# Projections that start before the norm is known: x times the norm's weights goes in, 1/rms scales what comes out

## What is computed

```python
def rms_norm(x, w):
    y = x * rsqrt(mean(x * x, axis=-1) + NORM_EPS)
    return y * w

# a hybrid layer (first block, twice)
z = rms_norm(x, norm_mix_w) @ w_in + b_in
ya = dilated attention of rope(z[q]), rope(z[k]), z[v]
yb = sigmoid(z[mo]) * normed(mlstm(silu(conv(z[mq, mk])), z[mv], z[mi], z[mf]))
x = x + (sigmoid(z[ga]) * (ya @ w_proj_att) + sigmoid(z[gb]) * (yb @ w_proj_mlstm)) @ w_out
x = x + square(relu(rms_norm(x, norm_mlp_w) @ w_ff1)) @ w_ff2

# the layer of the second block, on x = rms_norm(x, final_norm_w)
p = rms_norm(x, norm1_w) @ w_in            # z, xbc, dt, q, k, v, qi, ki, wi, u, gates
y_ssd = rms_norm(ssd(silu(conv(p[xbc])), softplus(p[dt])) * silu(p[z]), ssd_norm_w)
y_att = attention over the top 128 keys that qi, ki, wi choose
y_pool = windowed means of p[u], mixed
x = x + (sum of sigmoid(gates) * (y @ w_up)) @ w_out
hn = rms_norm(x, norm2_w);  a, b = split(hn @ w_ffn_in)
out = rms_norm(x + (silu(a) * b) @ w_ffn_out, final_norm_w)
```

## Time and profile before

| | |
|---|---|
| median of the runs | 2765.41 us (2763.36 to 2765.75, 3 runs) |
| the profiled execution | 2763.08 us, span 2761.3 us |
| mean granted clock of PE | 0.963 |
| busy: PE, DVE, ACT, POOL | 2640.0, 1102.0, 873.8, 955.9 us |
| HBM read and written | 213.81 and 2.10 MB, 78 GB/s |

### The profile page before, as it was taken

One profiled execution on the slowest core, in us unless ns is written; L12 is line 12 of the kernel. 1 busy time (PEld: TensorE's weight loads), 2 busy tenths in 40 slices (PEclk: granted clock), 3 DMA queues, 4 the chain that ended last, 5 costly groups with the idle time before them and its releaser, 6 DMA issues. The chain is left out here.

```text
span 2761.3 us, 30509 instructions
## 1 busy us (share of the span) xinstructions
PE 2640.0 (96%) x12181; PEld 2105.6 (76%) x12181; DVE 1102.0 (40%) x1490; ACT 873.8 (32%) x1087; POOL 955.9 (35%) x207
## 2 busy tenths in 40 slices
PE   7999999999998999899999998989899999999998
PEld 6757688788886857688788887778776588788887
DVE  3345543440513245544440422166666524322202
ACT  4245233321322245333331322352323423322212
POOL 2313234344442312334244443352232144344441
PEclk7999999999998999999999998999899999999999
DMA  3212122223322211122223322221111122223221
GB/s 130 77 31 75 59 81 92 76 91 100 99 91 70 92 31 62 61 77 92 76 91 97 101 91 77 77 77 54 52 61 61 50 92 92 77 92 105 91 98 54
DMA packets 176245, 217.90 MB, mean 79 GB/s; under 512 B 7564, under 2 KB 156996, under 8 KB 176132
## 3 DMA queue, kind: packets, MB, share of 16 engines
q1 hardware_dynamic: 175364, 215.66, 24.3%
q10 hardware_dynamic: 768, 0.66, 0.1%
HBM read 213.81 MB, written 2.10 MB: 78 GB/s over the span
## 5 line engine op out<-in xcount | busy, mean ns | idle before, releaser
L262 POOL TENSOR_TENSOR w_lo<-w_raw,w_hi 128x2048 fp32r<-128x2048 f32 x203 | 955.7, 4708 | 1765.7 <-ACT w_hi L253 1765.7
L253 ACT ACTIVATE w_hi<-w_raw 128x2048 fp32r<-128x2048 f32 x203 | 387.9, 1911 | 644.4 <-PE ps L1543 341.4
L292 PE MATMUL ps<-h_hi,w_hi 128*128 128x512 f32 x960 | 373.5, 389 | 0.0
L293 PE MATMUL ps<-h_lo,w_hi 128*128 128x512 f32 x960 | 373.5, 389 | 0.0
L294 PE MATMUL ps<-h_hi,w_lo 128*128 128x512 f32 x960 | 373.5, 389 | 0.0
L628 PE MATMUL ps<-h_hi,w_hi 128*128 128x512 f32 (+2 forms) x760 | 329.2, 433 | 1.3 <-issue 1.3
L628 PE MATMUL ps<-h_hi,w_lo 128*128 128x512 f32 (+2 forms) x760 | 302.9, 399 | 0.0
L628 PE MATMUL ps<-h_lo,w_hi 128*128 128x512 f32 (+2 forms) x760 | 302.2, 398 | 0.0
L292 PEld LDWEIGHTS ps<-h_hi,w_hi 128*128 128x128 f32 x960 | 180.2, 188 | 37.6
L294 PEld LDWEIGHTS ps<-h_hi,w_lo 128*128 128x128 f32 x960 | 180.2, 188 | 37.4
L293 PEld LDWEIGHTS ps<-h_lo,w_hi 128*128 128x128 f32 x960 | 180.2, 188 | 37.3
(11 more groups left out here) (404 smaller groups left out, 4134.4 us busy)
## 6 DMA issues: line engine op xcount, KB each, us to landing
w_raw<-in_w_in SPq DMA_DIRECT2D x74, 1024.0 KB, 5.2
w_raw<-in_w_ff SPq DMA_DIRECT2D x64, 1024.0 KB, 5.2
w_raw<-in_w_ffn_in SPq DMA_DIRECT2D x22, 1024.0 KB, 5.1
w_raw<-in_w_out SPq DMA_DIRECT2D x12, 1024.0 KB, 5.0
w_raw<-in_w_ffn_out SPq DMA_DIRECT2D x11, 1024.0 KB, 4.8
w_raw<-in_w_proj_att SPq DMA_DIRECT2D x4, 1024.0 KB, 5.2
w_raw<-in_w_proj_mlstm SPq DMA_DIRECT2D x4, 1024.0 KB, 5.0
w_raw<-in_w_up_ssd SPq DMA_DIRECT2D x4, 1024.0 KB, 5.1
```

Of the source, the lines that this page charges most:

```text
L253: act.activation(k.whi[:, slot * SLOT:(slot + 1) * SLOT], k.wraw[:, slot * SLOT:(slot + 1) * SLOT], ACT.Copy).then_inc(k.hi_done, 1)
L262: pool.tensor_tensor(k.wlo[:, a:a + SLOT], k.wraw[:, a:a + SLOT], k.whi[:, a:a + SLOT], ALU.subtract).then_inc(k.split, 1)
L292: pe.matmul(out, k.whi[:, w], xh(i), start=i == 0, stop=False)
L293: pe.matmul(out, k.whi[:, w], xl(i), start=False, stop=False)
```

## The change

Ten things, of which the first four are the core.

1. `Hand` takes the place of `Stats` and `Norm`. When a tile of x is final, ACT writes h_hi = x * w straight from it (L363) and its square (L373), and DVE writes h_lo = x * w - h_hi (L367). 1/rms is no part of h.
2. The squares of the eight tiles are added up on DVE (L381), through a PSUM bank. Four matmuls sum the one tile that is left, and one spreads 1/rms. Both are issued inside the side work that follows (`hooks`), not ahead of it. The spread result is kept as `rstd`, in the layout of tokens along columns, and as `rtok`, with tokens on partitions.
3. The lead unit is `fm_lead` (L316): 32 matmuls that need only h_hi, then the 16 with h_lo.
4. Evictions multiply by `rstd` or `rtok` on DVE. Where there is a bias or a tanh, it is a second instruction on ACT (`post`), which waits for DVE's. An MLP's `Up` takes relu times rstd out of PSUM on DVE and squares on ACT. `Glu` scales both halves on DVE and does silu on ACT in place.
5. `TwoNorms` does the two norms between the blocks at once: h_hi is x times the product of both weights, and the second mean square is a weighted sum of the same squares. `FirstNorm` scales x itself by the first norm, eight instructions on DVE ahead of the second block's conv.
6. `LastNorm` multiplies x by w as its tiles come; 1/rms goes on with the copies of the turned result.
7. `Project` is gone. q, k, v and the second block's conv inputs are side jobs like the others.
8. The loop, the clearing of semaphores and the barrier are gone: both layers are written out, and semaphores count on.
9. Setup: parameters are loaded and turned first; the four loads of x are issued by ACT. The bias of v is added to the attention's result, and the token biases are loaded from ACT's queue.
10. The ones of `mv` are written only where they are needed.

The number of units stays 203, and the budgets of the side work stay as they are. The core of the diff:

```diff
-class Stats(Stage):
-    def sum(self, pe, t):
-        pe.wait_ge(self.sem("squared"), t + 1)
-        for i in range(TT):
-            mm = pe.matmul(k.ps[:, self.bank, i:i + 1], self.slot(t)[:, i * P:(i + 1) * P], k.ones(P, 1), ...)
-class Norm(Stage):
...
+class Hand(Stage):
+    def hi(self, act, t):
+        act.wait_ge(*self.tile(t))
+        act.activation(self.k.hh(t), self.x(t), ACT.Copy, scale=self.w(t)).then_inc(self.sem("hi"), 1)
+    def lo(self, dve, t):
+        dve.wait_ge(*self.at("hi", t + 1))
+        dve.scalar_tensor_tensor(self.k.hl(t), self.x(t), self.w(t), self.k.hh(t), ALU.mult, ALU.subtract)\
+           .then_inc(self.sem("lo"), 1)
+    def add(self, dve, n):
+        t, ps = self.order[n], self.k.ps[:, self.ACC, :]
+        dve.wait_ge(*self.at("squared", max(t, self.seed) + 1))
...
+        out = self.acc if n == KD - 2 else ps
+        dve.tensor_tensor(out, ps, self.sq[t], ALU.add).then_inc(self.sem("added"), 1)
+    def sums(self, pe):
+        pe.wait_ge(*self.at("added", KD - 1))
+        for i in range(TT):
+            mm = pe.matmul(k.ps[:, self.SUMS, i:i + 1], self.acc[:, i * P:(i + 1) * P], k.ones(P, 1), ...)
...
+def fm_lead(k, pe, u, kt, cols, hand, outs, done):
+    for i in range(kt):
+        pe.wait_ge(*hand.at("hi", i + 1))
+        for c, out in enumerate(outs):
+            pe.matmul(out, k.whi[:, w], k.hh(i), start=i == 0, stop=False, skip_group_check=True)
+            pe.matmul(out, k.wlo[:, w], k.hh(i), start=False, stop=False, skip_group_check=True)
+    for c, out in enumerate(outs):
+        for i in range(kt):
+            if c == 0:
+                pe.wait_ge(*hand.at("lo", i + 1))
+            mm = pe.matmul(out, k.whi[:, w], k.hl(i), ...)
...
     def emit_out(self, who, eng, upto):
...
+                if job.post:
+                    eng.wait_ge(*self.read(job))
+                    job.post(eng).then_inc(self.sem("post"), 1)
...
     def conv_in(t):
-        return Job("act", lambda act, bank: act.activation(
-            cv[:, a:a + T], k.ps[:, bank, :], ACT.Identity, bias=k.col(B1 + 12 + t)), c=t % UT)
+        return biased(cv[:, a:a + T], t, B1 + 12 + t)
+    def scaled(dst, c, post=None):
+        return Job("dve", lambda dve, bank: dve.tensor_tensor(dst, k.ps[:, bank, :], rstd, ALU.mult), c=c % UT,
+                   post=post)
+    def biased(dst, c, bcol):
+        return scaled(dst, c, lambda act: act.activation(dst, dst, ACT.Identity, bias=k.col(c0 + bcol)))
...
     # Up, on ACT and on DVE
-            act.activation(r, k.ps[:, 2 * j:2 * j + 2, :].rearrange("p a b -> p (a b)"), ACT.Relu)\
-            dve.tensor_tensor(f, r, r, ALU.mult).then_inc(self.sem("f"), 1)
+            dve.scalar_tensor_tensor(r.rearrange("p (a b) -> p a b", b=T), k.ps[:, 2 * j:2 * j + 2, :], 0.0, rstd,
+                                     ALU.max, ALU.mult).then_inc(self.sem("r"), 1)
+            act.activation(f, r, ACT.Square).then_inc(self.sem("f"), 1)
...
+class FirstNorm(Stage):
+        for t in range(KD):
+            dve.scalar_tensor_tensor(h.x(t), h.x(t), h.w1(t), self.k.ps[:, h.FIRST, :], ALU.mult, ALU.mult)\
...
-            with nc.Fori(0, DEPTH) as l:
-                emit(k, first_layer(k, l, A))
+        x, angles = first_steps(k, A, table, st)
+        for l in range(DEPTH):
+            x = first_layer(k, l, A, st, x, angles)
+        second_layer(k, A, out, st, x)
+        emit(k, st)
```

More of the change, by code:

```diff
@@ L356, in act @@
     def act(self, act):
         k = self.k
[L358 to L362, removed]
+        if self.ahead is not None:
             hi_unit(k, act, self.ahead, 0)
-        act.wait_ge(self.sem("summed"), KD)
-        act.activation(k.root[:, 0:TT], k.ps[:, self.bank, 0:TT], ACT.Sqrt, bias=k.eps[:, 0:1],
+        act.activation(k.eps[:, 4:5], k.eps[:, 0:1], ACT.Sqrt)
+        act.wait_ge(*self.at("sums", 1))
@@ L366, in act @@
+        act.activation(k.root[:, 0:TT], k.ps[:, self.SUMS, 0:TT], ACT.Sqrt, bias=k.eps[:, 0:1],
                        scale=1.0 / D).then_inc(self.sem("root"), 1)
[L367 to L379 removed]
+        act.wait_ge(*self.at("recip", 1))
@@ L546, in unit @@
     def unit(self, src, kt, cols, xh, xl, jobs):
         u = units(self.k, 1)
+        lead = not self.units
         self.units.append((u, src, cols))
@@ L550, in unit @@
             job.n, job.u, job.kt, job.cols, job.xh, job.xl = len(self.jobs), u, kt, cols, xh, xl
-            job.last = job is jobs[-1]
+            job.last, job.lead = job is jobs[-1], lead
+            if job.n < 4:
+                job.need = [*job.need, self.before.tile(job.n)]
             if not job.last:
@@ L1230, in up @@
                 t = j * (w // P) + c
-                waits = [self.read(self.gates[t])] + (list(free) if t == 0 else [])
+                waits = [self.posted(self.gates[t])] + (list(free) if t == 0 else [])
                 if add:
@@ L1586, in dve @@
             if c < KD - 1:
[L1587 removed]
+                dve.wait_ge(*self.at("tile", c + 1))
             else:
@@ L2655, in second_layer @@
     dt_rows = k.at("s_dt_rows", o_scr + T, T)
-    dt_at = plain(DT2, SH, [Job("act", lambda act, bank: act.activation(
-        dt_rows[0:SH, :], k.ps[0:SH, bank, :], ACT.Copy), c=0, rows=SH)])
+    for j in range(6):
+        xbc_at = plain(XBC2 + j * UC, UC, [copy(xbc3[:, t, CONV - 1:], t % UT) for t in (2 * j, 2 * j + 1)])
+    side.hooks = {side.jobs[2].end: [hand.sums], side.jobs[3].end: [hand.spread]}
+    dt_at = plain(DT2, SH, [Job("dve", lambda dve, bank: scaled(dve, dt_rows[0:SH, :], bank, slice(0, SH)),
+                                c=0, rows=SH)])
     for j in range(4):
```

1537 lines of the change are left out of this document (821 added, 716 removed).

## The result

The changed kernel takes 2689.8 us (median of 4 runs, 2685.0 to 2691.7), the one before 2764.4 beside it: ratio 0.973, 95% interval 0.971 to 0.974. That is 75 us less where 89 were forecast; 2689.8 lies inside the range, 15 us above the forecast. The profiled execution took 2689.5 us with a span of 2687.7, so 73.6 us less than the span before.

The account below looks back on a forecast made before the run. PE was taken as the bound, its own sums and half clock at norms outweighing waits; 113 us gained at the norms less 24 lost in the middle gave 89, so 2675 us, eight times in ten 2645 to 2712.

Parts of the forecast that it names:

- Three norms before an MLP: Norms in both first layers and once in the second block: few sums left on PE, 39 us gained in all.
- End of layer 0: Norm after the first layer: 24.2 us of cost falls to 1.9 us of sums and spread, 22.3 us gained.
- Between the blocks: Two successive norms costing 40.4 us: 3.8 of sums and spreads and 1.8 of PE's wait stay, 34.8 us gained.
- Start: Kernel's beginning: lead unit ends at 45 instead of 53.2, 6.3 us gained, bounds 0 to 15.
- End: After the last product: turning back the result needs only x times w and begins at once, 11 us gained.
- lead units that don't run ahead: Rival: slots come free late, so five norms each wait 4.5 us for POOL's w_lo; 22 less gain, 2696 us, chance 0.08.
- evictions that POOL slows: Rival: about 120 moved evictions each cost 0.90 us more on DVE, kernel slower at 2782 us, chance 0.04.
- Rope: Two evictions on DVE ahead of the rotation PE waits for: 1.4 us lost per layer.
- The rest of the layers: Per layer, three output-gate evictions between conv taps lose 2.1 us, and some eight mLSTM gate evictions about 3.2.
- SSD: Four evictions in the tail of this second-block stage, on a wait of 4.5 us: 2.8 us lost.
- Attention and pooling: Second block's attention and pooling stretch: evictions moved to DVE would lose only 1 us.
- DVE's chains become the second bound: Rival: longer PE waits in rope, gates, mLSTM and conv, some followed by half clock; loss 50, 2700 us, chance 0.22.

## Why the prediction was right, and where it was off

- **PE's work and clock around the norms bound the kernel: right.** The waits as a whole didn't fall, and the gain is PE's busy time, 77.5 us. That the second half of a norm is dear through sums and the lower clock was shown by putting the sums back: 50 us.
- **Three norms before an MLP**, 39: measured 13.4, 13.4 and 11.8. The lo parts met POOL more often than foretold, once in each of the three norms and not once in all, but behind 32 products without h_lo that cost little: all six waits for h_lo come to 1.9 us.
- **End of layer 0**, 22.3: measured 22.3. The clock of 1.00 came as foretold.
- **Between the blocks**, 34.8: measured 35.1, with a wait of 1.50 where 1.8 was taken.
- **Start**, 6.3: measured 4.2. The second unit does start at 45.14 as foretold (53.17 - 45.14 = 8.0, less 1.9 for sums and spread), but PE then waits 1.90 us once more, for DVE's qk at 59.94. That the start came out as said is in part luck: the angles met both w_lo, a case that I had priced at no gain, and their operations were cheaper than my 0.7 us, most of them 0.43. Where rope begins, 2.8 us are left of it.
- **End**, 11: measured 12.0. Together the norms gave 112, with 113 forecast. The rivals on this side, lead units that don't run ahead and evictions that POOL slows, were wrong: the 56 gate evictions took 685 and 687 ns on average, by the groups below, and of all evictions with 1/rms the 26 that ran beside a w_lo took 671 to 693 ns, the 97 others 669 to 694.
- **Rope**, 1.4 per layer: measured 1.25. **The rest of the layers**, 5.3 each: measured 3.7 and 1.8. The eight evictions of the mLSTM cost nothing; its stretch is even 2.4 us shorter in both layers. What was lost came from elsewhere. From the forget gates to the softplus 2.9 us went in each layer: ACT's second pass over the output gates now waits for DVE, so its w_hi is late and PE waits for POOL's w_lo. And the attention took 3.1 and 1.3 us more. In the first layer that is the clock behind the longer wait of rope, 3.4 us for 2.2; the same place, after and before:

```profile
138.00:144.00 6.00, 6.00 (x15) 3.35 (x15) 2.19 (x8) 1.53 (x6) 0.00 (x0) 0.67 0.00 0
```

```profile
135.00:141.00 6.00, 6.00 (x22) 3.29 (x23) 2.30 (x11) 2.39 (x7) 0.00 (x0) 1.00 0.10 5
```

  The second layer's 1.3 are within the 2.8 us that came and went there without an edit.
- **Second conv**, 3.9: measured 0.8, since the scalings lay beside other work.
- **SSD**, 2.8: mis-sized, measured 6.2. The evictions were 2, and three, not four, stood in the tail; 4.2 was the collision of DVE's scaling with a w_lo that ACT's free time had moved there.
- **Gates in the rounds of top-k**, 3: measured 2.9.
- **"Attention and pooling, 1"**: this is the step that failed, with 23.3 us. I had counted how long the evictions take. But an eviction on DVE also waits for its products, and behind it, in order, stood the pooling that PE waits for; so late, it also met two w_lo with PE out of other work. Two experiments that take this meeting away give back 21 us each.

The groups of moved evictions, of the kernel after (busy, mean ns of one):

```profile
L1330 DVE TENSOR_TENSOR gate<-ps,rstd 128x512 f32<-128x512 f32 x32 | 21.9, 685 | 56.2 <-PE ps L706 56.2
L1330 DVE TENSOR_TENSOR s_gate<-ps,cos 128x512 f32<-128x512 f32 x24 | 16.5, 687 | 67.1 <-PE ps L706 65.6 <-issue 1.5
```

The losses come to 2.5 + 5.5 + 0.8 + 6.2 + 2.9 + 23.3 = 41.2, and putting the evictions back gives 40.6, an agreement that is part chance, since the stages differ. 112 - 41 = 71 stands against the measured 73.6 of the spans; some 3 us I can't place. The rival "DVE's chains become the second bound" came as near as my forecast, with a loss of 50 and 2700 us, 10 from the measured time where mine was 15 off. But it named rope, gates, mLSTM and conv, and these took 9 us of the loss.

## What to carry to other kernels

When an eviction moves to another engine, its 0.7 us is the smaller price: ask which products it waits for, and what stands behind it on that engine that the bound engine is waiting for. Here three such evictions, 2.1 us by their length, cost 22 us. Put evictions of side work behind the main chain's group, not ahead of it. And look for small matmuls on the bound engine first, since here they cost their own time and the clock of what followed.

## What the runs showed of the hardware

- The granted clock fell from 1.00 to 0.50 while PE did nothing but one-column fp32 matmuls, with no idle time in the rows; it was 1.00 again after 512-column products had followed. The prediction named two waits ahead of the low clock of the earlier trace rows; that such sums bring it down without a wait was not in it.
- Beside a w_lo on POOL, DVE operations on SBUF alone took 4.6 to 4.9 us instead of 0.43 and 0.69, also one with a single tile as input (L1907); one on 128x16 numbers (L2292, below) took 4.40 instead of 0.17. Evictions, with an operand in PSUM, took 0.69 there as elsewhere. The Trainium skill (SBUF — State Buffer, SBUF: two separate sides) names two kinds of VectorE operation, one with two SBUF inputs and one in a 2-port mode, that share a pair of ports with GpSimd, so that the later one is blocked until the first has finished. I had used only the first half of it. L1908 and L2292 have two SBUF inputs and agree; L1907 was held with one, which fits the second kind, though no trace here names an operation's mode.

```profile
2125.34 4.40 DVE L2292 TENSOR_TENSOR s_pooled<-s_window,s_u 128x16 f32<-128x16 f32 x1
```

- Freed time on ACT was no gain by itself: it moved POOL's w_lo to where DVE was on the path.
